# Two value tiles move to ScalarE, layer 0's taps are placed anew, and the first head's work runs in another order

## The chip, the cores and the metric

The kernel runs on one core of a Trainium2 chip, as one launch. The metric is the device time of the execution in microseconds; a lower number is better.

## The reference

Two transformer blocks run one after the other on x of 512 tokens and 1024 features, in float32. The first block has two layers, and the change lies in its mixer, which each layer runs once:

```
u = h @ w_in;  x_m, z, glu_a, glu_b = split(u)
x_c = silu(short causal convolution of x_m, 4 taps)
q = x_c w_q,  k = x_c w_k,  v = x_m w_v           (4 heads of 256)
gates = [q,k,v] w_gates -> input gate ig, forget gate lf = log_sigmoid(fg)
h_m = mLSTM(q, k, v, ig, lf), normed per head, times sigmoid(z)
a = glu_a * sigmoid(glu_b);  a = long causal convolution of a, 31 taps
a = silu(group norm of a over 8 groups)
y = [h_m, a] @ w_out
```

An MLP with squared ReLU follows in each layer. The second block (attention with selected keys and with a window, and an MLP) is not touched by the change.

## The kernel before, in words

All activations are kept with features on the 128 partitions and the 512 tokens along the free axis: eight tiles of 128x512 for 1024 features. Large products are made in three passes (`product`, L2505): each operand is split into a high part in fp32r and a low rest, and TensorE adds high*high, low*high and high*low. Weights come by DMA in chunks of 128x1024 into a ring of four slots; SyncE issues a chunk's transfer when the chunk four places ahead has been used. ScalarE makes a chunk's high part (`high_part`, L1076), and GpSimd its low part (`low_part`, L950), in the order of the chunks, three chunks ahead of TensorE. Activations are split in the same manner by ScalarE and VectorE.

Products are written to four PSUM banks in turn, `bank(o) = PB[o % 4]`. TensorE may write the tile `o` once somebody has taken tile `o - 4` out (`wait_bank`, `wait_taken`). Four more banks, PM[0] to PM[3], hold sums, broadcasts and running convolutions.

The order on each engine is written out by hand, and engines meet at semaphores. In a layer's mixer TensorE's order is: GLU chunks, x_m chunks, two value chunks (eight tiles, two for each head), two query chunks, two key chunks, the gate products mixed with transposes of the values, four pairs of chunks for z (`gate_product(0)` to `(7)`), then the heads, then the output product. Beside it:

- VectorE runs the long convolution (`long_conv`, `conv_pair`, L1884) for tiles 0, 1, 4, 5, 6 and 7, two tiles at a time, one multiply-add for each tap and tile. It is cut into pieces that stand between other work. The short convolution (`short_conv`) of each pair of x_m tiles stands there too. `cut` says at which tap of tiles 4 and 5 the pieces end that stand before each pair of x_m tiles. Tiles 2 and 3 are made by ScalarE (products with a tap, L1194) and GpSimd (their sums, L981).
- During the value products VectorE copies each value tile out of its bank (L2047) and makes the low parts of x_c (`xc_low`, L2010, two inputs from SBUF), in turn for each head. Query products need both parts of x_c; ScalarE makes the high parts (L1282).
- While TensorE works on z, VectorE's `bias_gates` (L2054) and `gate_rows` (L2059 to L2071) stand inside the last long convolution, at the taps given in `beside`. TensorE's transposes (L2827) between `gate_product(2)` and `gate_product(3)` wait for the last of them. ScalarE's `lsig` chain (L1309 to L1317) stands between the two.
- `conv_mean(t)` (L2806) sums a group, `centre_conv` (L2077) takes the mean off, ScalarE squares (L1321), `conv_vars` (L2582) sums the squares, ScalarE takes the root (L1103) after a table load, VectorE refines its inverse (`refine`, L1699 to L1692), `conv_spreads` (L2587) spreads it over partitions, `conv_normed` (L2131) multiplies, ScalarE applies SiLU (L1375) and splits (L1173), `conv_low` (L2136) makes the low part, and `conv_product` multiplies by w_out.
- For each head: `stabiliser` (L2851), `diagonal` (L2094), `decay` on ScalarE (L1349, L1352), `scores` (L2864), `weighted` on VectorE (L2103), `weighted_values` (L2880), GpSimd's sums of weighted scores (L1019), and `denominator` (L2582 again). GpSimd also centres the values (L1003) before the first head's products.

Some of ScalarE's functions need a table of their own; a row ACT_TABLE_LOAD stands where it changes.

## Time and profile before

| | |
|---|---|
| median of 3 runs | 2272.92 us (2271.24 to 2275.35) |
| the profiled execution | 2276.22 us |
| its span in the trace | 2274.4 us |
| TensorE busy | 2221.9 us, 98% |
| VectorE, ScalarE, GpSimd busy | 55%, 43%, 49% |
| mean granted TensorE clock | 0.993 of full speed |

The span runs from the first to the last instruction; 1.8 us of the execution lie around it. "Busy" counts every instruction from its start to its end, and consecutive matrix products overlap. In a timeline, a bracket at the end of a row gives the time for which the engine was idle just before it, and the event that came last before it started, which need not be the one that it waited for. A row with x2 or more joins neighbouring instructions of one kind.

### The profile page before, as it was taken

How to read it: one execution, taken by the hardware profiler on the slowest of the kernel's cores; microseconds unless marked ns; L12 is line 12 of the kernel's file. 1: busy time of each engine (PE TensorE's matmuls, PEld its weight loads, DVE VectorE, ACT ScalarE, POOL GpSimd, SP SyncE). 2: the span in 40 equal slices, each digit the busy share in tenths (PEclk: the TensorE clock that was granted, in tenths of full speed). 3: DMA queues.
4: the chain of work that ended last, by engine and by line, in shares of the span. 5: the costliest groups of instructions: out<-in, count | busy, mean ns of one | idle time of the engine just before them, and what ended most of it. 6: DMA issues, size and time to landing. Idle time of an engine off the chain costs nothing.

```text
span 2274.4 us, 28719 instructions
## 1 busy us (share of the span) xinstructions
PE 2221.9 (98%) x10450; PEld 1750.4 (77%) x10450; DVE 1248.2 (55%) x2077; ACT 985.0 (43%) x1614; POOL 1113.6 (49%) x596
## 2 busy tenths in 40 slices
PE   7999999999999999999999999999999999999998
PEld 5886667788888878766778888887767688888886
DVE  4989846863556599984464122147776653221222
ACT  3368543333133335775343223234666653331323
POOL 2688833544344648875364444363322244443442
PEclk9999999999999999999999999999999999999999
DMA  8432205354656323220222323332212123323232
GB/s 318 138 94 75 67 29 162 129 203 145 237 173 204 93 80 97 75 85 28 65 75 93 101 93 97 97 95 78 77 55 65 47 93 93 103 92 98 96 98 87
DMA packets 206662, 240.39 MB, mean 106 GB/s; under 512 B 9762, under 2 KB 172378, under 8 KB 206554
## 3 DMA queue, kind: packets, MB, share of 16 engines
q1 hardware_dynamic: 205990, 238.76, 33.0%
q8 instruction: 65, 1.06, 0.2%
q14 instruction: 43, 0.35, 0.1%
q10 hardware_dynamic: 564, 0.21, 0.0%
HBM read 236.84 MB, written 2.10 MB: 105 GB/s over the span
## 4 chain that ended last, share of the span: by engine, by line
PE 83%; DVE 7%; POOL 3%; ACT 3%; issue 2%; DMA 1%; ACTq 0%; DVEq 0%; POOLq 0%; SPq 0%
PE product L2507 25%; PE product L2509 25%; PE product L2508 25%; PE product L2880 1%; POOL ring_low L950 1%; PE side L2864 1%; PE side L3075 1%; POOL slot_f L981 1%; PE product L3110 1%; DVE side L1884 1%; PE side L3095 1%; POOL slot_f L1003 1%; DMA ring_f<-in_w_out 1%; ACT ring_high L1076 1%; DVE side L1672 1%
## 5 line engine op out<-in xcount | busy, mean ns | idle before, releaser
L950 POOL TENSOR_TENSOR ring_low<-ring_f,ring_high 128x1024 fp32r<-128x1024 f32 (+1 forms) x349 | 842.5, 2418 | 1045.6 <-ACT ring_high L1076 1045.0
L2507 PE MATMUL product<-slot_r,ring_high 128*128 128x512 f32 (+1 forms) x2536 | 1006.1, 397 | 14.0 <-POOL ring_low L950 6.0
L2509 PE MATMUL product<-slot_r,ring_high 128*128 128x512 f32 (+1 forms) x2536 | 989.2, 390 | 0.0
L2508 PE MATMUL product<-slot_r,ring_low 128*128 128x512 f32 (+1 forms) x2536 | 988.4, 390 | 0.0
L1076 ACT ACTIVATE ring_high<-ring_f 128x1024 fp32r<-128x1024 f32 (+1 forms) x349 | 367.7, 1056 | 707.4 <-DMA ring_f<-in_w_ff 329.9
L2507 PEld LDWEIGHTS product<-slot_r,ring_high 128*128 128x128 f32 (+1 forms) x2536 | 475.9, 188 | 143.7 <-issue 30.7
L2509 PEld LDWEIGHTS product<-slot_r,ring_high 128*128 128x128 f32 (+1 forms) x2536 | 475.9, 188 | 101.9
L2508 PEld LDWEIGHTS product<-slot_r,ring_low 128*128 128x128 f32 (+1 forms) x2536 | 476.3, 188 | 97.0 <-issue 1.4
L1884 DVE SCALAR_TENSOR_TENSOR side<-slot_f,cols,side 128x512 f32<-128x512 f32 x380 | 253.5, 749 | 0.6
L1842 DVE SCALAR_TENSOR_TENSOR va<-product,sqt 128x512 f32<-128x512 f32 x96 | 66.3, 692 | 333.3 <-ACT sqt L1154 332.0
L1862 DVE TENSOR_TENSOR slot_f<-product,slot_f 128x512 f32<-128x512 f32 x64 | 44.2, 690 | 175.1 <-PE product L2509 175.1
L1154 ACT ACTIVATE sqt<-product 128x512 f32<-128x512 f32 x96 | 57.0, 594 | 112.2 <-PE product L2509 111.3
L2507 PE MATMUL product<-ring_high,slot_r 128*128 128x512 f32 x256 | 99.6, 389 | 0.0
L2508 PE MATMUL product<-ring_high,slot_r 128*128 128x512 f32 x256 | 99.6, 389 | 0.0
L2509 PE MATMUL product<-ring_low,slot_r 128*128 128x512 f32 x256 | 99.6, 389 | 0.0
L2469 DVE SCALAR_TENSOR_TENSOR slot_f<-product,inv_cols,slot_f 128x512 f32<-128x512 f32 x32 | 22.8, 747 | 137.7 <-PE product L2509 137.7
L1672 DVE SCALAR_TENSOR_TENSOR side<-slot_f,cact,side 128x512 f32<-128x512 f32 x120 | 90.7, 756 | 4.8
L1834 DVE TENSOR_TENSOR slot_r<-va,slot_r 128x512 fp32r<-128x512 f32 x96 | 92.6, 974 | 0.2
L981 POOL TENSOR_TENSOR slot_f<-slot_f,sqt 128x512 f32<-128x512 f32 x60 | 77.9, 1320 | 9.6 <-ACT sqt L1194 9.6
L981 POOL TENSOR_TENSOR slot_f<-slot_f,va 128x512 f32<-128x512 f32 x60 | 80.2, 1359 | 4.6 <-ACT va L1194 4.6
L1169 ACT ACTIVATE slot_r<-va 128x512 fp32r<-128x512 f32 x96 | 60.1, 626 | 6.0 <-DVE va L1842 5.1
L1112 ACT ACTIVATE slot_f<-slot_f 128x512 f32<-128x512 f32 x32 | 20.2, 631 | 86.3 <-DVE slot_f L1862 45.8
(324 smaller groups left out, 2077.2 us busy)
## 6 DMA issues: line engine op xcount, KB each, us to landing
ring_f<-in_w_ff SPq DMA_DIRECT2D x128, 512.0 KB, 3.8
slot_f<-in_w_ada SPq DMA_DIRECT2D x48, 1024.0 KB, 7.2
ring_f<-in_w_in SPq DMA_DIRECT2D x96, 512.0 KB, 3.9
ring_f<-in_w_out SPq DMA_DIRECT2D x40, 512.0 KB, 3.4
ring_f<-in_w_up SPq DMA_DIRECT2D x32, 512.0 KB, 3.7
ring_f<-in_w_down SPq DMA_DIRECT2D x32, 512.0 KB, 3.7
slot_f<-in_x SPq DMA_DIRECT2D x4, 512.0 KB, 5.2
ring_f<-in_w_v SPq DMA_DIRECT2D x4, 512.0 KB, 3.5
```

The costliest lines, as they stand in the source:

```text
L950: pool.tensor_tensor(whole(ring_low[:, s, :, :], n), whole(ring_f[:, s, :, :], n), whole(ring_high[:, s, :, :], n).bitcast(F32), ALU.subtr ...
L981: pool.tensor_tensor(tile(SC, t), tile(SC, t), tap[u % 4], ALU.add).then_inc(tap_used.sem, 1)
L1076: act.activation(whole(ring_high[:, s, :, :], n), whole(ring_f[:, s, :, :], n), ACT.Copy).then_inc(high_ready.sem, 1)
L1154: act.activation(sqt[:, t % 2, :], bank(o0 + t)[:], ACT.Relu).then_inc(relu_ready.sem, 1)
L1169: act.activation(tile_r(SC, t), va[:, t % 2, :], ACT.Copy).then_inc(fh_ready.sem, 1)
L1672: ins = dve.scalar_tensor_tensor(ada_acc[:] if b and kk == 3 else PM[0][:], ada_raw(slot, b)[:, kk, :], c_col, PM[0][:], ALU.mult, ALU.add)
L1834: dve.tensor_tensor(tile_r(SD, t), va[:, t % 2, :], tile_r(SC, t).bitcast(F32), ALU.subtract).then_inc(fs_ready.sem, 1)
L1842: dve.scalar_tensor_tensor(va[:, t % 2, :], bank(o0 + t)[:], 0.0, sqt[:, t % 2, :], ALU.max, ALU.mult).then_inc(taken[(o0 + t) % 4].sem, 1)
L1884: ins = dve.scalar_tensor_tensor(sum_out, src(t, k, T), wk, running, ALU.mult, ALU.add)
L2507: pe.matmul(out_ap, high, rhs_high, start=start, stop=False)
L2508: pe.matmul(out_ap, low, rhs_high, start=False, stop=False)
L2509: return pe.matmul(out_ap, high, rhs_low, start=False, stop=stop)
```

## The change

It has three parts, and the code for both layers is the same except where l == 0 is asked.

1. ScalarE copies value tiles 0 and 1 out of their banks, with an instruction each in its loop over the first head; VectorE copies tiles 2 to 7 and stands `xc_low` of each pair behind the copies of the next pair.
2. In layer 0, 18 and not 14 taps of tiles 4 and 5 stand ahead of the values, and inside the convolution of tiles 6 and 7 the bias stands at tap 9 (was 2), the gate rows at 17 (was 9), and the centring of tiles 0 to 3 at 22 and 26 (was 14 and 18); tiles 4 and 5 are centred behind it.
3. The last two means stand ahead of `gate_product(7)`, both variances right behind it; ScalarE takes the root before its first exponentials; VectorE refines before the first head's weighting and mixes norming with it; the spreads stand between the first head's products, and use two banks for tiles 0 to 3 and two others for tiles 4 to 7, with the waits that this asks for.

```diff
         def spread_bank(t):
-            return (PB[2], PB[3], PM[2], PM[3])[t % 4]
+            return (PB if t < BLK else PM)[2 + t % 2]
...
                         ahead.of(place, I_V + hd // 2)
+                        if hd == 0:
+                            o = O_V + t
+                            wait_done(act, place, LAYER, o)
+                            wait_taken(act, place, O_XM + t)
+                            act.activation(xm(t, CONV_M - 1, T), bank(o)[:], ACT.Copy).then_inc(taken[o % 4].sem, 1)
...
+                    if t == 6:
+                        conv_square(6)
+                        conv_square(7)
                     act.activation(tile(SE, t), bank(o)[:], ACT.Sigmoid).then_inc(taken[o % 4].sem, 1)
...
                 taps.make(place, TAPS)
-                conv_square(6)
-                conv_square(7)
+                square_root_next()
+                wait(act, place, cvar, 2)
+                deviation(place, PM[2][:, 0:P], P, croot_ready)
...
                     decay(0, j)
-                square_root_next()
-                wait(act, place, cvar, 2)
-                deviation(place, PM[2][:, 0:P], P, croot_ready)
...
-                    long_conv(place, 4, 0, 4)
+                    long_conv(place, 4, 0, 5)
...
-                cut = (4, 11, 13, 14, 14, 17) if l == 0 else (12, 19, 22, 24, 26, 28)
+                cut = (5, 12, 14, 16, 18) if l == 0 else (12, 19, 22, 24, 26)
...
-                for hd in range(HEADS):
+                for hd in range(1, HEADS):
                     for t in (2 * hd, 2 * hd + 1):
                         o = O_V + t
                         wait_done(dve, place, LAYER, o)
                         dve.tensor_copy(xm(t, CONV_M - 1, T), bank(o)[:]).then_inc(taken[o % 4].sem, 1)
-                    xc_low(2 * hd, 2 * hd + 1)
+                    xc_low(2 * hd - 2, 2 * hd - 1)
+                xc_low(6, 7)
...
-                    long_conv(place, 6, beside={2: bias_gates, 9: gate_rows, 14: lambda: centre_conv(0, 1),
-                                                18: lambda: centre_conv(2, 3), 22: lambda: centre_conv(4, 5)})
+                    long_conv(place, 6, beside={9: bias_gates, 17: gate_rows, 22: lambda: centre_conv(0, 1),
+                                                26: lambda: centre_conv(2, 3)})
+                    centre_conv(4, 5)
...
                 diagonal(0)
-                weighted(0, 0)
-                weighted(0, 1)
                 wait(dve, place, croot_ready, 1)
                 settled(dve)
                 refine(PM[2], P, P, crn_small)
+                weighted(0, 0)
+                weighted(0, 1)
                 wait(dve, place, cxc_ready, NT)
+                conv_normed(0, 1)
                 weighted(0, 2)
+                conv_normed(2, 3)
                 weighted(0, 3)
-                conv_normed(0, 1, 2, 3)
...
                 gate_product(6)
-                gate_product(7)
                 conv_mean(6)
                 conv_mean(7)
+                gate_product(7)
                 conv_vars(0)
+                conv_vars(1)
...
-                        elif t < 4:
+                        elif t in (4, 5):
                             wait(pe, place, p_ready, BLK)
                         else:
-                            wait(pe, place, cy_ready, t - 3)
+                            wait(pe, place, cy_ready, t - 1)
...
                     if c == 0:
-                        wait(pe, place, cy_ready, NT - 2)
+                        wait(pe, place, cy_ready, BLK)
...
                 stabiliser(0)
-                conv_vars(1)
                 scores(0, 0)
                 scores(0, 1)
+                conv_spreads(0)
...
                 scores(0, 2)
+                conv_spreads(2)
                 weighted_values(0, 1)
                 scores(0, 3)
-                conv_spreads(0)
                 weighted_values(0, 2)
-                conv_spreads(2)
                 stabiliser(1)
                 conv_spreads(4)
```

## Rows read from the trace of the kernel before

**Rows 1.** The page, part 1: busy us (share of the span), instructions.

```profile
PE 2221.9 (98%) x10450; PEld 1750.4 (77%) x10450; DVE 1248.2 (55%) x2077; ACT 985.0 (43%) x1614; POOL 1113.6 (49%) x596
```

**Rows 2.** TensorE's waits: us in total, times, longest.

```profile
PE product L2507 <- POOL ring_low L950: 6.0, 3, 2.8
PE side L2582 <- POOL slot_f L1019: 3.4, 2, 1.7
```

**Rows 3.** Timeline of TensorE, layer 0: start us, us, what, idle before and releaser.

```profile
178.67 0.47 PE L2507 MATMUL product<-slot_r,ring_high 128*128 128x512 f32 x1 [2.75 <-POOL ring_low L950]
...
188.20 0.50 PE L2507 MATMUL product<-slot_r,ring_high 128*128 128x512 f32 x1 [1.09 <-DVE slot_f L2047]
...
198.76 0.39 PE L2508 MATMUL product<-slot_r,ring_low 128*128 128x512 f32 x1
...
199.89 0.39 PE L2507 MATMUL product<-slot_r,ring_high 128*128 128x512 f32 x1
...
238.01 0.38 PE L2827 MATMUL side<-ident,slot_f 4*128 4x4 f32 x4 [0.64 <-DVE floor_rows L2071]
...
272.18 1.98 PE L2806 MATMUL side<-slot_f,ones 128*128 128x512 f32 x4 [1.04 <-DVE slot_f L1884]
...
277.16 3.27 PE L2864 MATMUL side<-slot_f 128*128 128x512 f32 x8
...
291.07 0.43 PE L2582 MATMUL side<-slot_f,one_hot 128*32 128x128 f32 x8
...
309.42 0.43 PE L2582 MATMUL side<-slot_f,one_hot 128*32 128x128 f32 x8 [1.72 <-POOL slot_f L1019]
```

**Rows 4.** Timeline of ScalarE, layer 0.

```profile
174.23 1.06 ACT L1076 ACTIVATE ring_high<-ring_f 128x1024 fp32r<-128x1024 f32 x1
...
188.21 1.06 ACT L1076 ACTIVATE ring_high<-ring_f 128x1024 fp32r<-128x1024 f32 x1 [2.62 <-DMA ring_f<-in_w_k]
189.17 1.07 ACT L1287 ACTIVATE slot_f<-product 128x512 f32<-128x512 f32 x2
...
294.14 0.82 ACT L1375 ACTIVATE slot_f<-slot_f,cols 128x512 f32<-128x512 f32 x1 [0.20 <-DVE slot_f L2131]
```

**Rows 5.** Timeline of VectorE, layer 0.

```profile
160.90 0.69 DVE L2004 TENSOR_TENSOR slot_r<-product,slot_r 128x512 fp32r<-128x512 f32 x1 [2.03 <-ACT slot_r L1268]
...
183.93 3.61 DVE L2010 TENSOR_TENSOR slot_r<-slot_f,slot_r 128x512 fp32r<-128x512 f32 x2
...
283.84 0.29 DVE L1692 SCALAR_TENSOR_TENSOR inv_cols<-side,inv_cols 128x128 f32<-128x128 f32 x1
```

**Rows 6.** Timeline of GpSimd, layer 0.

```profile
182.89 2.41 POOL L950 TENSOR_TENSOR ring_low<-ring_f,ring_high 128x1024 fp32r<-128x1024 f32 x1 [1.32 <-ACT ring_high L1076]
...
189.34 2.86 POOL L950 TENSOR_TENSOR ring_low<-ring_f,ring_high 128x1024 fp32r<-128x1024 f32 x1 [0.67 <-ACT ring_high L1076]
```

**Rows 7.** Timeline of VectorE, layer 0, long convolution and gate rows.

```profile
189.87 21.16 DVE L1884 SCALAR_TENSOR_TENSOR side<-slot_f,cols,side 128x512 f32<-128x512 f32 x32
...
218.02 0.75 DVE L2054 TENSOR_SCALAR slot_f<-side,small 128x512 f32<-128x512 f32 x1 [2.81 <-PE product L2765]
...
230.31 0.69 DVE L2059 SCALAR_TENSOR_TENSOR side<-side,slot_f 4x512 f32<-4x512 f32 x1 [2.31 <-ACT slot_f L1317]
...
234.73 3.13 DVE L2071 TENSOR_TENSOR floor_rows<-slot_f,ada_acc 4x128 f32<-4x128 f32 x4
```

**Rows 8.** Timeline of VectorE, layer 1.

```profile
950.08 3.49 DVE L2010 TENSOR_TENSOR slot_r<-slot_f,slot_r 128x512 fp32r<-128x512 f32 x2
...
991.67 0.69 DVE L2059 SCALAR_TENSOR_TENSOR side<-side,slot_f 4x512 f32<-4x512 f32 x1 [4.28 <-ACT slot_f L1317]
```

**Rows 9.** Windows: busy us (instructions) per engine, granted clock, DMA.

```profile
175.00:178.50 3.50, 0.91 (x5) 0.41 (x3) 3.47 (x7) 2.18 (x5) 3.50 (x3) 1.00 0.32 111
...
1672.20:1675.60 3.40, 1.04 (x8) 0.47 (x8) 2.76 (x10) 0.52 (x3) 0.00 (x0) 1.00 0.00 0
1675.60:1679.10 3.50, 3.50 (x13) 2.59 (x13) 3.21 (x17) 2.77 (x9) 1.04 (x1) 0.51 0.00 0
```

## The prediction

> **What bounds the kernel.** I read the page first, then TensorE's list of waits, then the timelines of TensorE, ScalarE, VectorE and GpSimd around each wait in the mixer. TensorE is busy for 2221.9 us, 98% of the span [rows 1], so 52.5 us is all that any reordering could remove, and most of that lies outside the mixer. The list's longest wait inside the layers [rows 2] is 6.0 us in three pieces, and the others come once per layer like it. Placed in time in layer 0 [rows 3] they are five: 2.75 us before the second chunk of value products (start 178.67), 1.09 us in the first query chunk (188.20), 0.64 us before the turned input-gate rows (238.01), 1.04 us before the last two group means (272.18), and 1.72 us before head 1's denominator (309.42). Layer 1 repeats the pattern, without the wait for the means. About 15 us is the most that this change can touch, 0.65% of the span.
>
> The label "ring_low L950" on the 2.75 us is not the cause. The chunk used there was split long before; the product also needs product bank 0, which holds value tile 0, and VectorE, which has the short convolution ahead of it in its order, copies it out about 0.1 us before TensorE starts. In the same way 1.09 us waits for value tile 6.
>
> **Value tiles.** ScalarE ends the split that starts at 174.23 (1.06 us) [rows 4] and can copy tile 0 at about 175.2, for 0.60 us (two of its copies from a bank, L1287, take 1.07). TensorE restarts at 175.9 in place of 178.67: -2.74. Tile 1 follows inside ScalarE's wait for the short convolution, so nothing behind it moves. VectorE copies tiles 2 and 3 where it copied 0 and 1, so everything on it moves up by one pair, and the second wait goes: -1.37 from start to start (its first half began at 184.11, a tile is 6 matmuls, five starts take 1.13 us [rows 3], so two tiles take 2.72 us, so the second half was due at 186.83 and began at 188.20).
>
> Then two new waits. First, query tile 4 needs bank 0 from ScalarE, whose copy of query tile 0 (0.96 us behind the start of the split at 188.21 [rows 4]) stands behind that split, and the split behind a weight transfer that is issued when a value chunk ends. All of it moves by the same 2.74 us, to 187.1; TensorE wants the bank at 186.8: +0.34. Second, the rows of VectorE's xc_low (L2010), which subtracts SBUF from SBUF: two of them take 3.61 us in place of 1.3 [rows 5]. The first begins at 183.93 while GpSimd's split of 182.89 runs (2.41 us, [rows 6]) and ends about 0.55 us after that one does; GpSimd's next instruction then gives way once, and so on by turns. In layer 0 the last two escape it, because GpSimd's next split only begins at 189.34, when VectorE is nearly done. After the change VectorE reaches those two 1.2 us earlier, and the split is ready at 186.6, so GpSimd starts it as soon as its tap sums end, at 188.6. By the turns of these rows xc_low(6) ends at 189.2, the split at 191.5 and xc_low(7) at 192.05. Layer 1 already shows this: its last pair takes 3.49 us [rows 8]. Query tile 6 needs that last tile at 190.55: +1.5. What stands behind it on VectorE is the rest of the long convolution. Sum of this block: -2.74 - 1.37 + 0.34 + 1.6 = -2.2 us in each layer. The bounds of the third wait are 0 and 2.3.
>
> The Trainium skill (GPSIMD Engine Reference, Key points) says that GpSimd and VectorE contend where a VectorE instruction has two SBUF inputs; by that page both engines may slow, and it does not say who goes first, which the rows do. By it the block gives less than 4.1 us; the rows give 2.2.
>
> **Layer 0's taps.** One pair of taps costs 1.32 us (32 instructions in 21.16 us, [rows 7]). Four pairs go ahead of the values: into VectorE's wait for the fourth GLU pair, and into the waits for ScalarE's high parts, of which one is the 2.03 us before 160.90 [rows 5] and the next is as long; each has room, so they cost nothing, and if one did not fit it would delay a copy by at most 0.6. The work behind the values falls from 17 to 13 pairs. But the input-gate rows now stand at tap 17, not 9, and the bias at 9, not 2. VectorE before: from 189.87, 26 pairs, the bias, waits of 2.81 and 2.31, and the rows of 230.31 to 237.86 (7.56 us) [rows 7]. After: from 192.05, 30 pairs (39.6), the bias (0.67), no wait, 7.56: ready at 239.9, and TensorE's L2827 at 240.06 in place of 238.01. TensorE comes there 2.2 us earlier, at 235.2. So the gain of layer 0's value block is not only lost, the path is 2.05 us later. If xc_low were not held, this work would start 1.2 us before 189.87, the two copies that left VectorE, and L2827 stand at 236.6; the bounds are -1.4 and +2.05. I take +2.05, since layer 1's row has the very pattern.
>
> TensorE then stands for 4.85 us in one piece. The clock fell to 1.2 GHz (0.51 of full) behind a stretch with 1.04 of 3.40 us busy, and not behind the 2.75 us wait [rows 9]. 4.85 us is longer than either, so I count one such stretch at half speed, about 1.7 us; the bounds are 0 and 1.7. The Trainium skill (TensorE: Matmul & The Clock Gate, Part 1) says that an idle TensorE drops to 1.2 GHz by itself. By it the 1.7 stands; without it the whole sum would be -0.3.
>
> Layer 1 keeps its order of taps. There VectorE stands idle for 4.28 us before the same rows [rows 8], waiting for ScalarE's logarithm, which hangs on TensorE; so layer 1 keeps its -2.2.
>
> **Means ahead of the last gate product.** Layer 0's convolution ends 8 pairs (10.5 us) nearer to the gate rows, so the means wait for nothing: -1.04. Both variances now run back to back; 0.25 more is saved where the last mean no longer drains alone. In layer 1 nothing waited: -0.05. Scores so start 1.3 us earlier against L2827 in layer 0.
>
> **First head.** I count from the start of the scores (277.16 [rows 3], S). Before, the block ends with the denominator at 291.07 (0.43 us), S+14.3 [rows 3]. After, the root, its table load (1.28 us) and the variances lie ahead of the exponentials; VectorE refines (five small instructions, 2.14 us up to the end of L1692, which starts at 283.84, [rows 5]) right behind its diagonal, S+1.33 to S+3.5. Scores end at S+3.11, so the first spreads wait 0.5. The spreads of tiles 4 to 7 now share two banks: the last pair waits for tile 5 to be normed. Following VectorE (0.60 us from one such instruction to the next) that is S+14.9, against TensorE's S+13.4: 1.5 more. The block ends at S+16.3: +2.0. But behind it the old chain went on to a wait of 1.72 us for GpSimd's sums: ScalarE's last SiLU ends at 294.96 [rows 4], S+17.8, then its exponentials, its split, GpSimd's split and sums. After, the last SiLU ends at S+19.0, and the chain gives the denominator at S+33.3, against S+32.26 before. TensorE's own work is there at S+32.1. So +1.05 in layer 0, and with -1.3 at S this stage is -0.25. Layer 1's denominator waits for the same sums [rows 2], and stands 0.85 us deeper in its stage, S+33.2; to S+33.3, with the -0.05, is about +0.15 with rounding. Each is good to 0.8.
>
> **Sum.** Layer 0: +2.05 + 1.7 - 0.25 = +3.5. Layer 1: -2.2 + 0.15 = -2.05. Together +1.45 us on this execution's 2276.22 (span 2274.4), which is 3.3 above the median 2272.92; so the median goes to 2274.4.
>
> **Rivals.** *VectorE is not held.* If GpSimd's split meets no xc_low, layer 1 gains 2.2 + 1.6 = 3.8 and layer 0 gains the 1.4 of the bounds, with a stand of 3 us and the clock kept: -1.4 - 0.25 - 3.8 + 0.15 = -5.3 us, 2267.6. For it: in layer 0 the last two were not held. Against it: the split that missed them comes earlier, and layer 1 held its last pair [rows 8].
>
> *The first head loses its order (slower).* Place: the last spreads, which wait for the fifth normed tile, in both layers. If ScalarE's chain does not absorb the 2.0 us, because the 1.72 us wait behind it stays whole, each layer pays 2.0 and not 1.05 (layer 0: +0.7, layer 1: +2.0): 2.05 + 1.7 + 0.7 - 2.2 + 2.0 = +4.3, and with one more hop of 0.6 late per layer +5.5: 2278.4. It decides from a last SiLU later than S+20.2. For it: each normed tile waits for a spread, and each spread for a normed tile. Against it: the terms are short.
>
> **From these to numbers.** My forecast has 0.55, the first rival 0.26, the second 0.19. A measurement of this kernel tells 0.2%, 4.5 us, from no change. So faster 0.26, same 0.55, slower 0.19. The forecast's own range is -3 to +4.5 us; with the rivals' prices, 2267.5 to 2278.5.
>
> **What would show it.** Right: ScalarE copies two value tiles at 175 and 177 and the 2.75 us wait is under 0.4; the last L2010 of layer 0 takes near 2.9 us and a query product waits over 1 us; L2827 waits 3 to 5 us in layer 0 for L2071 and under 1 in layer 1; no wait before the means; L2587 waits twice. Wrong: L2827 of layer 0 starting before 237.5, the clock at 1.00 behind it, or the denominator's wait gone.

## The result, and the profile after

The change makes the kernel slower: 2290.43 us against 2275.35 us (medians of five executions each), ratio 1.0060 with a 95% interval of 1.0049 to 1.0071. The prediction said 2274.4 us and a range up to 2278.5; it counted from 2272.92 us, the median of the three executions then at hand, and forecast +1.5 us where +15.1 came. The ratios in this document are made from the single executions and not from the medians; the two ways differ by up to 1.4 us. The profiled execution takes 2291.05 us (span 2289.3) against 2276.22 (span 2274.4).

Line numbers move by 5 to 10: L2507 to L2509 are now L2516 to L2518, L2010 is L2016, L2071 is L2078, L2827 is L2836, L2587 is L2596, L2880 is L2890.

The page of the changed kernel, part 1, answers to [rows 1]:

```profile
PE 2235.0 (98%) x10450; PEld 1760.4 (77%) x10450; DVE 1252.4 (55%) x2073; ACT 986.3 (43%) x1618; POOL 1116.2 (49%) x596
```

TensorE has the same 10450 matmuls and is busy for 13.1 us more, of the 14.9 us by which the span grew; it is idle for 54.3 us where it was 52.5. Work that did not grow but takes longer ran at a lower clock: the mean granted clock is 0.985 against 0.993, some 34 us more at half clock. So in this pair the waits that the change adds and those that it removes nearly cancel, and almost all of the loss is clock. Its list of waits (total, times, longest) answers to [rows 2]:

```profile
PE side L2836 <- DVE floor_rows L2078: 9.0, 2, 8.4
...
PE side L2596 <- DVE slot_f L2139: 2.9, 2, 1.4
PE product L2516 <- DVE slot_r L2016: 2.8, 2, 1.4
...
PE product L2890 <- DVE slot_f L2111: 2.1, 2, 1.5
...
PE product L2516 <- POOL ring_low L950: 0.5, 1, 0.5
```

The two waits of 2.75 us for the value tiles are gone (of the 6.0 us only the third, 0.5, is left), and the denominator's 3.4 us are gone from the list. In their place stand one wait of 8.4 us, two of 1.4 us before the last spreads, and 2.1 us in two before head 1's value products (L2890). TensorE's timeline in layer 0 answers to [rows 3]. The whole trace of after runs 1.5 us ahead of before from the first microseconds on, where before has a stretch at half clock at 20 us that after has not; this is no effect of the change.

```profile
190.59 0.50 PE L2516 MATMUL product<-slot_r,ring_high 128*128 128x512 f32 x1 [1.38 <-DVE slot_r L2016]
...
233.24 0.39 PE L2518 MATMUL product<-slot_r,ring_high 128*128 128x512 f32 x1
242.05 0.24 PE L2836 MATMUL side<-ident,slot_f 4*128 4x4 f32 x1 [8.42 <-DVE floor_rows L2078]
...
285.41 1.16 PE L2596 MATMUL product<-inv_cols,row_pick 32*128 32x128 f32 x16 [0.35 <-DVE inv_cols L1698]
297.25 1.76 PE L2596 MATMUL side<-inv_cols,row_pick 32*128 32x128 f32 x16 [1.43 <-DVE slot_f L2139]
316.51 1.57 PE L2890 MATMUL product<-slot_f 128*128 128x256 f32 x8 [0.58 <-DVE slot_f L2111]
```

Why the floor rows are late shows in the timelines of VectorE and, below it, of GpSimd; they answer to [rows 7] and [rows 6]:

```profile
230.85 0.68 DVE L2066 SCALAR_TENSOR_TENSOR side<-side,slot_f 4x512 f32<-4x512 f32 x1
231.56 1.21 DVE L2068 TENSOR_TENSOR_SCAN slot_f<-ones,side 4x512 f32<-4x512 f32 x1
232.80 0.68 DVE L2072 TENSOR_TENSOR slot_f<-side,slot_f 4x512 f32<-4x512 f32 x1
233.51 1.21 DVE L2074 TENSOR_TENSOR_SCAN ada_acc<-slot_f 4x512 f32<-4x512 f32 x1
234.76 7.14 DVE L2078 TENSOR_TENSOR floor_rows<-slot_f,ada_acc 4x128 f32<-4x128 f32 x4
```

```profile
234.22 2.65 POOL L950 TENSOR_TENSOR ring_low<-ring_f,ring_high 128x1024 fp32r<-128x1024 f32 x1 [1.78 <-ACT ring_high L1076]
236.84 2.57 POOL L981 TENSOR_TENSOR slot_f<-slot_f,sqt 128x512 f32<-128x512 f32 x2
239.37 2.38 POOL L950 TENSOR_TENSOR ring_low<-ring_f,ring_high 128x1024 fp32r<-128x1024 f32 x1
```

Four additions on [4 x 128] end one by one at 237.01, 238.28, 239.55 and 241.90, each just behind a GpSimd instruction. Before, the same four took 3.13 us [rows 7]: 1.20 and 1.28 us for the first two, held in the same way, and 0.28 and 0.29 us for the last two, since GpSimd happened to stand idle for 1.78 us from 237.09 us on.

The windows show what a wait does to the clock (busy us of TensorE, weight loads, VectorE, ScalarE and GpSimd, then the granted clock and DMA). They answer to [rows 9]:

```profile
232.80:236.20 3.40, 0.82 (x4) 0.36 (x2) 3.33 (x3) 2.77 (x4) 1.98 (x1) 1.00 0.31 86
236.20:239.60 3.40, 0.00 (x0) 0.00 (x0) 3.31 (x4) 0.00 (x0) 3.40 (x4) 0.50 0.19 68
239.60:243.00 3.40, 0.95 (x5) 0.97 (x6) 3.40 (x3) 0.00 (x0) 3.40 (x3) 0.50 0.00 0
243.00:246.40 3.40, 3.40 (x9) 2.63 (x9) 3.40 (x6) 0.00 (x0) 1.27 (x2) 0.50 0.00 0
...
294.20:297.60 3.40, 1.97 (x25) 1.69 (x25) 2.39 (x4) 1.66 (x3) 0.00 (x0) 1.00 0.00 0
297.60:301.00 3.40, 3.40 (x27) 2.50 (x25) 2.12 (x5) 1.29 (x3) 0.00 (x0) 0.50 0.02 5
```

The clock falls to 1.2 GHz at 236.2 us, within the wait of 8.42 us, and stays there to 246.4 us. Behind the 1.43 us it falls too, from 297.6 to 304.5 us, with TensorE busy for 1.97 of 3.40 us ahead of it. Layer 1 has stretches of 3.4 us, at 1062 us behind its 1.43 us and at 1079 us behind its 1.50 us:

```profile
1058.80:1062.20 3.40, 1.97 (x27) 1.61 (x27) 2.69 (x6) 2.09 (x4) 0.00 (x0) 1.00 0.00 0
1062.20:1065.60 3.40, 3.40 (x10) 2.65 (x9) 3.07 (x8) 3.00 (x5) 0.00 (x0) 0.50 0.00 0
```

Landmarks of TensorE, after minus before, give the account of the profiled pair, in us. Start of the trace -1.5; layer 0's values -2.2; turned gate rows +7.7; clock behind them +2.0; up to the scores -1.4; first head, up to head 2's scores, +4.0; up to layer 1 +1.1; its values -2.0; its first head +4.0; the rest of layer 1 +4.7; from there to the end -1.5. Sum +14.9. Single profiles differ by themselves: outside the code that the change touches, the half-clock stretches at 434, 803 and 1199 us are 6.8 us each where before has 3.4, and before has one at 1676 us, of 3.4, that after has not. Each such step is 1.7 us, so differences of that size between two profiles prove nothing.

### The profile page after: what moved, and what is told of

The parts are those of the page before. It is cut to its first block, busy times and chain, and to the rows that moved or that the text cites. A ratio compares the mean times of both kernels' runs of the same rounds, so it can differ in the third digit from the quotient of the medians.

```text
span 2289.3 us, 28727 instructions
## 1 busy us (share of the span) xinstructions
PE 2235.0 (98%) x10450; PEld 1760.4 (77%) x10450; DVE 1252.4 (55%) x2073; ACT 986.3 (43%) x1618; POOL 1116.2 (49%) x596
## 3 DMA queue, kind: packets, MB, share of 16 engines
q8 instruction: 65, 1.06, 0.2%
## 4 chain that ended last, share of the span: by engine, by line
PE 86%; DVE 8%; ACT 2%; DMA 1%; issue 1%; POOL 0%; SPq 0%; DVEq 0%; ACTq 0%; POOLq 0%
PE product L2516 26%; PE product L2518 25%; PE product L2517 25%; DVE side L1890 2%; PE product L2890 1%; PE side L2874 1%; PE product L2602 1%; PE side L3084 1%; DVE slot_r L2016 1%; PE product L3119 1%; DMA ring_f<-in_w_out 1%; PE side L3104 1%; PE side L2815 1%; DMA slot_f<-in_w_ada 1%; DVE side L1678 1%
## 5 line engine op out<-in xcount | busy, mean ns | idle before, releaser
L2516 PE MATMUL product<-slot_r,ring_high 128*128 128x512 f32 (+1 forms) x2536 | 1010.8, 399 | 7.6 <-DVE slot_r L2016 2.8
L2518 PE MATMUL product<-slot_r,ring_high 128*128 128x512 f32 (+1 forms) x2536 | 991.3, 391 | 0.0
L2516 PEld LDWEIGHTS product<-slot_r,ring_high 128*128 128x128 f32 (+1 forms) x2536 | 477.6, 188 | 137.1 <-issue 31.6
L2518 PEld LDWEIGHTS product<-slot_r,ring_high 128*128 128x128 f32 (+1 forms) x2536 | 477.2, 188 | 102.3
L1890 DVE SCALAR_TENSOR_TENSOR side<-slot_f,cols,side 128x512 f32<-128x512 f32 x380 | 253.5, 749 | 0.6
L2516 PE MATMUL product<-ring_high,slot_r 128*128 128x512 f32 x256 | 99.6, 389 | 0.0
L2518 PE MATMUL product<-ring_low,slot_r 128*128 128x512 f32 x256 | 99.6, 389 | 0.0
L1112 ACT ACTIVATE slot_f<-slot_f 128x512 f32<-128x512 f32 x32 | 20.2, 631 | 86.2 <-DVE slot_f L1868 45.6
```

The costliest lines, as they stand in the source:

```text
L1890: ins = dve.scalar_tensor_tensor(sum_out, src(t, k, T), wk, running, ALU.mult, ALU.add)
L2516: pe.matmul(out_ap, high, rhs_high, start=start, stop=False)
L2518: return pe.matmul(out_ap, high, rhs_low, start=False, stop=stop)
```

## The experiments

All medians below are of five or more executions, beside runs of the kernel before on the same chip (2275.85 us beside the first three, 2277.09 beside the next four, 2275.82 beside the next four, 2276.57 beside the last two). An earlier form of the release in part 2, with a semaphore of its own behind the a row, gave no time. Edits are shown against the changed kernel where nothing else is said.

### Which part of the change costs

**Parts 1 and 2 (values and taps), everything of the means and the first head as before.**

```
                 gate_product(6)
+                gate_product(7)
                 conv_mean(6)
                 conv_mean(7)
-                gate_product(7)
                 conv_vars(0)
-                conv_vars(1)
...
```

> The changed kernel without its third part: the means, the root and the first head in their old order; value tiles by ScalarE and the taps of layer 0 as changed. Theory A+B (stand and first head share the loss): the landmarks of the two traces show 4.0 us (layer 0) and 4.1 us (layer 1) gained by time between the start of the scores and head 2's scores; without the new order these go, the wait before the last means (1 us) comes back: about 2283 us against 2290. Theory A alone, with the first head priced as predicted (near zero): 2290. The stand before the turned gate rows stays at 8 us in both.

Measured: 2280.28 us, ratio 1.0023 (1.0014 to 1.0033), 3 us below the first theory and far from the second. The stand before the turned gate rows is 8.5 us, as in the full change, and no half-clock stretch is left in either first head.

**Part 3 alone (means, root and first head in the new order) on the kernel before.**

> The kernel before with the third part alone (means ahead of the last gate product, root, variances and spreads of the first head in the new order). As predicted: -1.3 at the scores, +1.05 and about +0.85 behind them, so within 1 us of before, 2275. Theory B (each spread that waits 1.4 us or more also drops the clock for 3.4 to 6.8 us): two falls of the clock that before does not have, +6 to +8 us, 2281 to 2283.

Measured: 2293.06 us, ratio 1.0075 (1.0061 to 1.0088), worse than the whole change and far beyond either theory. A part of it was expected by neither: with the taps in their old places the convolution is not ready for means that stand 5.7 us earlier.

```profile
271.28 3.78 PE L2808 MATMUL side<-slot_f,ones 128*128 128x512 f32 x4 [6.48 <-DVE slot_f L1885]
```

The clock is at 1.2 GHz for 10.2 us around it (the four mean products take 3.78 us where they took 1.98 in [rows 3]). So the third part needs the second. Not all of the 17 us is its own, though. This kernel has the wait of 2.75 us for value tile 0 unchanged, and here the clock falls behind it in both layers, for 3.4 us each, where it stayed at 1.00 in [rows 9]:

```profile
177.40 0.47 PE L2509 MATMUL product<-slot_r,ring_high 128*128 128x512 f32 x1 [2.75 <-POOL ring_low L950]
```

```profile
174.60:178.10 3.50, 0.75 (x4) 0.64 (x4) 3.46 (x7) 2.20 (x5) 3.25 (x2) 1.00 0.48 150
178.10:181.50 3.40, 3.40 (x10) 2.64 (x9) 3.40 (x7) 3.40 (x6) 1.78 (x1) 0.50 0.00 0
```

**The first head's order alone** takes the means out of this (and puts ScalarE's last two squares, which go with them, back). Against part 3 alone:

```
                 gate_product(6)
+                gate_product(7)
                 conv_mean(6)
                 conv_mean(7)
-                gate_product(7)
                 conv_vars(0)
...
```

> The kernel before with the new order of the first head alone (spreads of tiles 0 to 3 ahead of value products, root and variances ahead, spreads of tiles 4 to 7 in two banks); the last means stay behind the last gate product. The third part alone measured 1.0075, of which 6.5 us of wait before the means and 10.2 us at half clock belong to the means. Theory: what is left is the head's own cost, 3 to 4 us a layer, 1.003 of before, 2282 us. Rival (as predicted, +1 us a layer): 2277.

Measured: 2284.69 us, ratio 1.0042 (1.0028 to 1.0056). The head's order costs 8.9 us in two layers, not 1 a layer. Its profile has the two waits of 1.43 us that the prediction named, two more that it did not name (1.06 and 1.61 us, before head 1's value products), and at or behind each of the four a stretch at half clock, 17 us in all, that it did not price. The first:

```profile
288.10:291.50 3.40, 2.28 (x22) 1.56 (x18) 1.73 (x3) 1.21 (x3) 0.14 (x1) 1.00 0.00 0
291.50:294.90 3.40, 3.09 (x25) 2.51 (x26) 1.77 (x4) 1.33 (x3) 0.00 (x0) 0.50 0.02 5
```

**Part 1 alone (value tiles 0 and 1 by ScalarE),** against the kernel before.

```
+                        if hd == 0:
...
+                            act.activation(xm(t, CONV_M - 1, T), bank(o)[:], ACT.Copy)
...
-                for hd in range(HEADS):
+                for hd in range(1, HEADS):
...
```

> The kernel before with the first part alone: ScalarE copies value tiles 0 and 1, VectorE the other six; taps and heads in their old places. As predicted the value block gives 2.2 us in each layer, and in layer 0 VectorE's waits of 2.81 and 2.31 us ahead of the gate rows take up its later start, so that the gate rows move with TensorE: -4.4 us, 2271. Rival C (the additions of the floor rows meet GpSimd's splits here too, or the clock takes it back): 2274 to 2277.

Measured: 2271.69 us, ratio 0.9980 (0.9971 to 0.9989), -4.2 us. This part does what was predicted, with waits of 1.25 and 1.37 us left for the held xc_low.

In us of the medians: part 1 gives 4.2, part 2 on top of it costs 8.6, part 3 on top of both 10.7 (15.1 less 4.4). By the ratios it is 4.6, 9.8 and 8.4, so which of the two parts costs more is not settled. The rest of the runs ask how.

### Part 2: why gate rows at tap 17 cost more than their place

**Floor rows added once and copied four times**, with TensorE's wait unchanged:

```
+                    steps.did(dve.tensor_tensor(gu, gb, max_row, ALU.add))
+                    steps.wait()
                     for s in range(BLK):
-                        block_s = slice(s * P, (s + 1) * P)
-                        dve.tensor_tensor(floor_rows[32 * s:32 * s + HEADS, :], gb[:, block_s], max_row[:, block_s],
-                                          ALU.add).then_inc(mrow_ready.sem, 1)
+                        dve.tensor_copy(floor_rows[32 * s:32 * s + HEADS, :],
+                                        gu[:, s * P:(s + 1) * P]).then_inc(mrow_ready.sem, 1)
```

> The changed kernel; VectorE adds all 512 columns of the floor rows in one instruction with two SBUF inputs, and four copies with one SBUF input put them in their places, in the place of four additions with two SBUF inputs. Theory (GpSimd holds each VectorE instruction that has two SBUF inputs until its own has ended, and no other): the addition takes up to 2.9 us, each copy 0.2 to 0.3, together 2 to 4 us in place of 7.14 in layer 0, the stand falls from 8.4 to about 5 us: 2286 to 2288 us. Rival (GpSimd slows every instruction of VectorE on SBUF): four copies take as long as the additions, 2290 to 2292.

Measured: 2289.53 us, ratio 1.0058 (1.0044 to 1.0072): no gain. My theory of two SBUF inputs fell short. The copies, min/median/max ns and first and last start, are held as well:

```profile
L2079 DVE COPY floor_rows<-slot_f x8: 216/1180/2267, 236.8 to 1009.4; 4x128 f32<-4x128 f32 x8
```

Three of the eight, 0.22 us each, ran with GpSimd idle; the five beside it took 1.17 to 2.27 us. In layer 0 the one addition takes 2.65 us and the four copies 5.92 us together, again one for each GpSimd instruction; the stand grows to 9.8 us. The rival as I wrote it (every instruction on SBUF) is not right either: the taps (L1890), which read one tile from SBUF and one from a bank, take 0.75 us both in 324 cases with a GpSimd instruction under way and in 56 without (changed kernel). VectorE's copies from a bank (L2053) take 0.68 us beside GpSimd too. The Trainium skill (SBUF — State Buffer, "SBUF: two separate sides") says that GpSimd and VectorE share one pair of ports, that a VectorE instruction with two SBUF inputs, or one in a 2-port mode, as a copy in fp32 from SBUF to SBUF is, needs it, and that who starts first holds it to its end. By that rule such a copy is held, and the trace agrees, by 1.17 us or more against 0.22.

**TensorE released in front of the floor rows.** The turned rows need only the a row, which the scan of L2074 is done with at 234.7 us.

```
                     steps.did(dve.tensor_tensor_scan(max_row, a_row, a_row, 0.0, ALU.max, ALU.max))
                     steps.wait()
+                    dve.sem_inc(mrow_ready.sem, 1)
...
-                wait(pe, place, mrow_ready, BLK)
+                wait(pe, place, mrow_ready, 1)
...
```

> The changed kernel, but TensorE's turned input-gate rows wait for the scan in front of the four floor rows and not for the floor rows (head 0's stabiliser and the sigmoid of gate tile 6 wait for those). Theory A: the scan ends at 234.8 us in layer 0, the floor rows at 241.9; the stand falls from 8.42 to about 1.2 us, and the 10.2 us at half clock behind it go: -7.2 and some -3 us, 2280 us against 2290. Rival (the time is given back at the group means, where TensorE then waits for VectorE's convolution): a wait of 3 us or more before L2812's counterpart, 2284 or more.

Measured: 2285.62 us, ratio 1.0041 (1.0027 to 1.0055). The stand falls to 1.2 us and the stretch at 236 us goes, yet of the 10 us expected only 4.3 come back by the ratios, 6.5 by the medians, each less its own kernel before; the two intervals just overlap. The mechanism of the rival was right (the time is given back later) and its place wrong: TensorE waits 1.3 us for a centring before an earlier mean, nothing before the last two, and 3.4 us at the first value product, for the centred values of GpSimd (L1003), with 6.8 us at half clock there.

**The same with the old first head**, the last means still ahead of the last gate product.

> The changed kernel with the release of the run before, and with the first head, the root and the variances in their old order; the last means still stand ahead of the last gate product. If the first head's new order is the larger part of the loss and the gate rows the rest, both are gone: value block -2.2 us in each layer, gate-row waits -0.6 in each, means -1.0: 2269 us, the fastest so far. Rival (the means wait for the convolution, or a clock fall comes back somewhere): 2274.

Measured: 2280.30 us, ratio 1.0019 (1.0010 to 1.0028), slower than the theory and the rival. The nearest kernel without the release, parts 1 and 2, measured 2280.28 us (it differs in the place of the last means too), although 7 us of stand are gone here. They stand elsewhere. TensorE, ScalarE and GpSimd of this kernel:

```profile
282.59 1.92 PE L2891 MATMUL product<-slot_f 128*128 128x512 f32 x2 [4.76 <-POOL slot_f L1003]
```

```profile
249.62 1.23 ACT L1326 ACTIVATE slot_f<-slot_f 128x512 f32<-128x512 f32 x2 [7.78 <-DVE slot_f L2086]
256.08 1.23 ACT L1326 ACTIVATE slot_f<-slot_f 128x512 f32<-128x512 f32 x2 [5.24 <-DVE slot_f L2086]
257.22 1.04 ACT L1076 ACTIVATE ring_high<-ring_f 128x1024 fp32r<-128x1024 f32 x1
```

```profile
258.33 2.41 POOL L950 TENSOR_TENSOR ring_low<-ring_f,ring_high 128x1024 fp32r<-128x1024 f32 x1 [11.30 <-ACT ring_high L1076]
260.71 0.28 POOL L998 TENSOR_SCALAR small<-small 128x16 f32<-128x16 f32 x1
261.08 3.63 POOL L1003 TENSOR_SCALAR slot_f<-slot_f,small 128x256 f32<-128x256 f32 x4
...
278.92 3.62 POOL L1003 TENSOR_SCALAR slot_f<-slot_f,small 128x256 f32<-128x256 f32 x4
```

Read from the bottom: GpSimd centres the last values until 282.5 us. It has four rounds of a split and four centrings, 24 us without a gap, and starts them at 258.33, after 11.3 us of idling for ScalarE's split. ScalarE makes that split at 257.22, behind squares of centred tiles 0 to 3, which waited 7.78 and 5.24 us for VectorE's centring. That centring is what the second part moved from taps 14 and 18 to 22 and 26. So the part delayed two things, and the first hid the second.

**Squares later**, to break that chain and nothing else, against the run before this one:

```
-                    if t in (3, 5):
-                        for u in {3: range(0, 4), 5: (4, 5)}[t]:
+                    if t == 5:
+                        for u in range(6):
                             conv_square(u)
```

> The run with the old head and the release, but ScalarE squares centred tiles 0 to 3 behind gate tile 5 and not behind gate tile 3, so that its splits of weights do not stand behind squares that wait for VectorE's centring at taps 22 and 26. Theory (late centring holds ScalarE's squares, these its split, that GpSimd's split and the centring of the values behind it; TensorE then waits 4.8 us at the first value product, L1003's centring): the wait falls below 1 us and the half-clock stretch at 283 us goes, -5 to -6.5 us: 2274 to 2275 us, 0.999 of before. Rival (GpSimd itself is the bound there, whatever ScalarE does): the wait stays over 3 us, 2280.

Measured: 2270.80 us, ratio 0.9980 (0.9971 to 0.9989). GpSimd starts centring at 249.4 us and ends at 277.8:

```profile
249.38 3.63 POOL L1003 TENSOR_SCALAR slot_f<-slot_f,small 128x256 f32<-128x256 f32 x4
...
274.21 3.61 POOL L1003 TENSOR_SCALAR slot_f<-slot_f,small 128x256 f32<-128x256 f32 x4
```

Of the 4.8 us wait 0.4 is left, and the half-clock stretch is gone. The gain, 9.5 us on the medians and 9 after the kernels before beside them, is larger than the 5 to 6.5 expected. 4.4 us of wait and half of 3.4 us are 6.1. In the profiles two later half-clock stretches, at 424 and 793 us, are 3.4 us each where the run before had 6.8; that is another 3.4 us, outside the code that was edited, and whether it belongs to the edit is not shown.

**Gate rows at tap 12, centring at 17, 21 and 25**, four pairs of taps still ahead of the values; first in the full change, then with the release and with head and means in their old places, then with the means ahead again:

```
-                    long_conv(place, 6, beside={9: bias_gates, 17: gate_rows, 22: lambda: centre_conv(0, 1),
-                                                26: lambda: centre_conv(2, 3)})
-                    centre_conv(4, 5)
+                    long_conv(place, 6, beside={4: bias_gates, 12: gate_rows, 17: lambda: centre_conv(0, 1),
+                                                21: lambda: centre_conv(2, 3), 25: lambda: centre_conv(4, 5)})
```

> The changed kernel in full, but with layer 0's bias at tap 4, gate rows at tap 12 and centring at 17, 21 and 25. Adding up the runs so far: the second part costs 9.6 us (parts 1 and 2 measure 1.0023, part 1 alone 0.998), and with the gate rows in reach of TensorE this goes; the third part's share stays: 2281 us, about 1.002. Rival (the third part needs the late convolution's order and gives the time back at the means): over 2286.

> Value tiles by ScalarE and four pairs of layer 0's taps ahead of the values, as in the change, but the bias at tap 4 and the gate rows at tap 12, where VectorE gets to them at about 214 and 226 us, just as TensorE and ScalarE have their inputs ready; centring five taps behind them, as before; release behind the scan; means and first head as before. Theory (the loss of the second part is the late place of gate rows and centring, which hold TensorE at 242 us and, through ScalarE's squares, its weight splits and GpSimd's centring of the values, again at the first head): both waits go, the waits before the turned gate rows (1.3 us in two layers) and before the last means (1.0) too; 4.4 + 1.3 + 1.0 less than before, 2269 to 2270 us. Rival (a late step elsewhere takes it): no better than the first part alone, 0.998 of before.

> The run before, with the last two means also ahead of the last gate product, as in the change. The means come 5.7 us sooner than in the run before; VectorE's last taps end about 4 us sooner than in the kernel before, which waited 1.04 us there. So a wait of 2 to 3 us comes before the means in layer 0, and a fall of the clock behind it: 2 to 5 us slower than the run before. Rival (VectorE is early enough): the same as the run before.

Measured: 2281.45 us in the full change, ratio 1.0027 (1.0016 to 1.0037), so 7.5 us (ratios) to 9.5 us (medians) of its loss are this placement of gate rows and centring. With the old head, the old means and the release 2270.26 us, ratio 0.9977 (0.9968 to 0.9987). With the means also ahead 2273.81 us, ratio 0.9991 (0.9981 to 1.0000), a wait of 2.5 us before the means in layer 0 and 3.4 us at half clock behind it: 3.5 us slower, as expected. All three came out within 0.5 us of the numbers expected or inside their range. But 0.9977 is not told apart from the 0.9980 of part 1 alone, which was the second run's rival: that the earlier taps and the release add anything to part 1 is not shown.

**The second of them with the squares later**, the lowest time of all:

> The fastest run so far (gate rows at tap 12, old head, release behind the scan) with the same change to the squares. There the wait for GpSimd's centring is 0.6 us a layer. Theory: it goes, and nothing else does, 0 to -1.2 us: 2269 to 2270 us. Rival (the squares, made later, hold the variances): 2271 or more.

Measured: 2268.54 us, ratio 0.9966 (0.9956 to 0.9976): 8 us faster than the kernel before and 22 faster than the changed one. From the run without this step it is not told apart, since the intervals overlap. Of the change it keeps the value tiles on ScalarE and four pairs of taps ahead of the values; means and first head are the old ones. What stays is 1.39 us a layer for the held xc_low, and 1.7 for the denominator.

### Part 3: a wait of 1.43 us that costs more than 1.43 us

**Work put into the wait.** Head 1's stabiliser moves between the spreads of tiles 4 and 5 and of tiles 6 and 7, and its product is computed twice.

```
-                stabiliser(1)
                 conv_spreads(4)
                 weighted_values(0, 3)
+                wait(pe, place, w_ready, 4)
+                pe.matmul(PM[0][:], neg_ident[:, 1:2].to_broadcast([HEADS, P]), max_row, start=True, stop=True)
+                stabiliser(1)
                 conv_spreads(6)
```

> The changed kernel; head 1's stabiliser product moves from ahead of the spreads of tiles 4 and 5 to ahead of those of tiles 6 and 7, and is computed twice there, so that TensorE has about 1.2 us of work in the wait of 1.43 us for tile 5's norm (one of the two products is work that does not count). Clock theory (the wait itself costs 1.4 us a layer, and the fall of the clock behind it 1.7 to 3.4 us more): the half-clock stretches of 6.8 us at 297 us and of 3.4 us at 1062 us go, 2284 to 2286 us against 2290. Rival (the falls have nothing to do with this wait): 2290 to 2291.

Measured: 2287.91 us, ratio 1.0049 (1.0035 to 1.0062), 2.5 us less than the change, with overlapping intervals, where 4 to 6 were expected. In layer 1 the fall at 1062 us is gone. In layer 0 the wait is gone and the clock falls all the same, for 3.4 us in place of 6.8:

```profile
295.20:298.60 3.40, 3.40 (x31) 2.13 (x31) 2.69 (x6) 2.04 (x3) 0.00 (x0) 1.00 0.02 5
298.60:302.00 3.40, 3.40 (x9) 2.62 (x8) 3.07 (x9) 2.88 (x5) 0.00 (x0) 0.50 0.00 0
...
1058.50:1062.00 3.50, 3.50 (x32) 2.24 (x32) 2.80 (x5) 2.04 (x3) 0.00 (x0) 1.00 0.00 0
```

And layer 0 gives the other 3.4 us back a little later: the wait before head 1's value products is 1.52 us where the change had 0.58, and the clock falls behind it, which it did not there.

```profile
315.51 2.81 PE L2890 MATMUL product<-slot_f 128*128 128x256 f32 x8 [1.52 <-DVE slot_f L2111]
```

```profile
312.30:315.70 3.40, 1.88 (x8) 0.90 (x7) 3.40 (x6) 0.00 (x0) 1.84 (x3) 1.00 0.00 0
315.70:319.10 3.40, 3.40 (x17) 2.44 (x17) 0.99 (x4) 2.22 (x7) 3.26 (x3) 0.50 0.01 2
```

So the clock theory is borne out in layer 1, and in layer 0 it is not: the fall came without the wait, and the sum at half clock stayed 6.8 us. A rival, that the run of small products (on 4 and 32 rows) in the new order drops the clock whether or not a wait stands in it, is left open. For it: layer 0 of this run. What the profiles do show is the place. All six kernels with the new head and no filling have 1.43 us before the last spreads in each layer, and in all twelve places the clock falls at that wait or within 2.1 us behind it. In no kernel with the old head does a fall begin at the spreads. But waits as long stand elsewhere and keep the clock: 24 before a query product (1.25 to 1.43 us, in the twelve kernels with part 1) and 16 before head 1's denominator (1.72 to 1.74 us, in the eight with the old head).

## Why the prediction was wrong, point by point

**The value tiles: right.** ScalarE copies the two tiles at 173.6 and 174.7 us, the 2.75 us wait and the second one are gone, xc_low(7) takes 2.87 us, and a query product waits 1.38 us (predicted 1.5). TensorE is 2.2 us earlier in layer 0 and 2.0 in layer 1 (predicted 2.2); part 1 alone measures -4.2 against -4.4. The rival in which VectorE is not held is refuted. (Two of the small sums did not close in the text: query tile 6 is +1.5 where it is read and +1.6 where it is summed, and layer 1's head comes to 0.05, not 0.15. Neither matters.)

**"No wait, 7.56: ready at 239.9": mis-sized.** Put on the time of before (plus 1.5), TensorE arrives at 235.1 (predicted 235.2), and the rows are ready at 243.4, not at 239.9. The floor rows take 7.14 us, not 3.13. VectorE reached the gate rows when predicted (230.85 plus 1.5, against 232.3). I took the sum of the four additions as a price of its own, in the same text that explained how GpSimd holds xc_low by turns. The 3.13 us in [rows 7] were already two held additions and two free ones, and at the new place none is free.

**"One such stretch at half speed, about 1.7 us": mis-sized.** The stretch is 10.2 us, 4.4 of them with work in them, and costs 2.0 to 2.2. Term and cost are close, by some luck: the stand was 8.4 us and not 4.85, and most of the longer stretch fell into it.

**The centring, which moves with the gate rows: left out.** ScalarE squares the centred tiles in front of its splits, and GpSimd centres the values behind them. In the changed kernel the long stand hides this. The release uncovers it as 3.4 to 4.8 us, and the run with later squares shows the chain.

**Means ahead: right.** No wait before them, and 1.4 us by the scores (predicted 1.3). The stand did not help it: with the release, which takes the stand away, the last two means wait for nothing either. With the gate rows at tap 12 they wait 2.5 us.

**The first head, "-0.25 and +0.15": the step that failed most.** Both waits came as priced (0.35 for 0.5, 1.43 for 1.5), and TensorE reached the last spreads 0.6 us later than predicted. What failed is the clock behind them. The prediction let two new waits of this length pass and put the clock there at nothing, where the landmarks give +4.0 us in each layer against -0.25 (with the -1.3 of the means in it) and +0.15. Layer 0 loses half of 6.8 us at half clock: 1.8 of waits, 3.4 of clock and 0.6 late, less the 1.72 that went before the denominator, is 4.1, against 4.0 measured. The one reading at hand, 2.75 us of [rows 9] with the clock at 1.00, could not carry that: the same wait dropped the clock in both layers of the run with part 3 alone. The chain behind the block failed too. Head 1's denominator starts at S+36.2 (318.01 us) and not at S+33.3, and its wait is gone, which the prediction had named as a sign of being wrong; and before head 1's value products there are new waits, 0.58 and 1.50 us, of which it had none. The rival "slower" named the right place and a price of 4.3 to 5.5 in sum, of the whole change; the head's order alone measures 8.9. Its test, a last SiLU later than S+20.2, did not decide: it ends at S+19.9.

**What stays open.** 4.7 us of the profiled pair arise in the rest of layer 1. 1.6 of them are a weight transfer that lands 5.2 us behind its issue and not 3.7, so that ScalarE's root, queued behind that chunk's split, is late; behind the wait of 2.18 us the clock is at half for 6.8 us. The runs with part 1 alone, with the first release and with the filled wait have such a wait (2.2, 2.0 and 1.8 us), those with parts 1 and 2, with part 3 alone and with the head alone have not. Since the run with part 1 alone has it, the new head is not needed for it, but I can't tell whether it belongs to the change. The same holds for the length of the half-clock stretches at the boundaries, 3.4 or 6.8 us without a pattern that I could find. Why the clock falls in the new first head, by the wait or by the small products around it, is not shown either.

## What to carry to other kernels

Before an instruction is moved in one engine's order, list what the other engines have at the new place: a chunk whose rows look cheap may be cheap only because GpSimd paused there. When TensorE is 98% busy, price each new wait of TensorE both with and without a fall of the clock behind it. In the first head here a wait of 1.4 us cost 1.7 or 3.4 us more; before a query product a wait of the same length cost nothing more. One profile in which a wait kept the clock is no proof that it will. And look for a signal that releases it earlier than the last instruction of a group. When a removed stand gives nothing back, follow the next wait back through every queue: it may have been there all along.

## What the runs showed of the hardware

The length of a wait did not foretell TensorE's clock. The same wait of 2.75 us at the same place kept 1.00 in two kernels (before, 0.91 of the 3.50 us around it busy [rows 9], and with the head alone) and was followed by 3.4 us at 1.2 GHz in a third (part 3 alone, 0.75 of 3.50 busy), in both layers each time. The same wait of 2.5 us before the last means kept it in one kernel (the full change with gate rows at tap 12) and not in another (gate rows at tap 12 with the means ahead). Waits of 1.43 us in the new first head had a fall in twelve of twelve places, waits of 1.25 to 1.43 us before a query product in none of 24. The fifteen kernels profiled give no rule that would foretell single cases.

Spreads and stabilisers that fill the record (3.40 of 3.40 us busy) lost the clock in one layer and kept it in the other.

VectorE's SBUF-to-SBUF copies of [4 x 128] are held by GpSimd just as additions with two SBUF inputs are: 1.17 to 2.27 us in five cases against 0.22 in three alone.
